# Expert value rows summed on TensorE in four 64x64 parts of the array, and more of them

## The reference

```python
vals, idx = lax.top_k(sc, PEER_TOPK)
...
experts = jnp.take_along_axis(cand_idx.reshape(...), top_c, axis=-1)
g = jax.nn.softmax(top_s, axis=-1)
ue = peer_u[experts]
ve = peer_v[experts]
act = jax.nn.gelu(jnp.einsum('td,thkd->thk', hc, ue).astype(jnp.float32), approximate=False)
return jnp.einsum('thk,thkd->td', (g * act).astype(ve.dtype), ve)
```

## Time and profile before

| | |
|---|---|
| Runs | 2926.47, 2927.46 (median), 2927.74 us |
| Profiled execution | one of these executions: span 2927.4 us, which lies within the three runs; next to nothing lies around it |
| Busy: PE, PEld | 2491.4 us (85%), 1743.2 us (60%) |
| Busy: DVE, ACT, POOL | 1760.7 us (60%), 1133.8 us (39%), 676.9 us (23%) |
| DMA | 838.64 MB, mean 286 GB/s |
| First dot product, last V row's sum | 567.2 us, some 2312 us |
| Before, in and behind the expert stage | 567, 1748 and 612 us |

### The profile page before, as it was taken

One profiled execution on the slowest core, in us unless ns is written; L12 is line 12 of the kernel. 1 busy time (PEld: TensorE's weight loads), 2 busy tenths in 40 slices (PEclk: granted clock), 3 DMA queues, 4 the chain that ended last, 5 costly groups with the idle time before them and its releaser, 6 DMA issues.

```text
span 2927.4 us, 29566 instructions
## 1 busy us (share of the span) xinstructions
PE 2491.4 (85%) x10118; PEld 1743.2 (60%) x10118; DVE 1760.7 (60%) x4222; ACT 1133.8 (39%) x2762; POOL 676.9 (23%) x566
## 2 busy tenths in 40 slices
PE   8999999879989759888968678588985799988998
PEld 7786666667755437546736544264763376655883
DVE  2101311598797778666989888878998416412430
ACT  2101301242533765354442578464554325512210
POOL 0000000122234343332223445444223101100000
PEclk9999999989989889999989578799997999999999
DMA  5545243689999999999899989999999743432443
GB/s 197 173 154 168 95 144 129 219 335 351 390 394 417 409 397 392 419 389 384 299 332 402 365 301 385 396 420 419 417 418 416 277 159 109 151 130 88 153 155 116
DMA packets 160966, 838.64 MB, mean 286 GB/s; under 512 B 17400, under 2 KB 21896, under 8 KB 95024
## 3 DMA queue, kind: packets, MB, share of 16 engines
q0 software_dynamic: 73728, 536.90, 45.8%
q1 hardware_dynamic: 82464, 287.75, 28.0%
q10 hardware_dynamic: 4624, 12.11, 1.1%
HBM read 828.27 MB, written 8.41 MB: 286 GB/s over the span
## 4 chain that ended last, share of the span: by engine, by line
PE 55%; DVE 18%; ACT 12%; DMA 11%; issue 4%; POOL 0%; ACTq 0%; DVEq 0%; SPq 0%
PE ps L908 26%; DMA BIG<-in_uv,BIG 10%; PE ps L928 5%; PE ps L929 5%; PE ps L1152 5%; DVE BIG L1943 5%; DVE X L1923 4%; PE ps L909 4%; PE ps L1176 2%; PE ps L1177 2%; ACT L1441 2%; DVE BIG L1854 1%; PE ps L1122 1%; DVE BIG L1851 1%; PE ps L1101 1%
## 5 line engine op out<-in xcount | busy, mean ns | idle before, releaser
L2160 POOL DMA_INDIRECT BIG<-in_uv,BIG x512 | 634.2, 1239 | 1646.3 <-DVE BIG L1900 564.6
L908 PE MATMUL ps<-BIG,RING 128*128 128x256 f32 x3472 | 807.6, 385 | 13.8 <-DMA RING<-in_w_cq 4.9
L908 PEld LDWEIGHTS ps<-BIG,RING 128*128 128x128 f32 x3472 | 670.1, 194 | 133.4 <-issue 28.6
L1943 DVE CUSTOM_DVE_ANT_0 BIG<-BIG 128x1024 f32<-128x1024 f32 x512 | 619.6, 1217 | 85.4 <-DMA BIG<-in_uv,BIG 84.2
L1923 DVE SCALAR_TENSOR_TENSOR X<-BIG,small,X 128x1024 f32<-128x1024 f32 x333 | 426.6, 1281 | 91.7 <-ACT small L1445 91.6
L1441 ACT ACTIVATE small<-small 128x1 f32<-128x1 f32 x512 | 102.6, 200 | 620.7 <-DVE small L1943 619.4
L908 PE MATMUL ps<-WK,RING 128*128 128x256 f32 x1232 | 287.2, 385 | 25.2 <-DVE BIG L1702 23.2
L908 PEld LDWEIGHTS ps<-WK,RING 128*128 128x128 f32 x1232 | 235.7, 193 | 65.3 <-DVE BIG L1702 31.1
L928 PE MATMUL ps<-RING,BIG 128*128 128x512 f32 (+1 forms) x448 | 223.0, 579 | 5.0 <-DVE BIG L1681 2.4
L929 PE MATMUL ps<-RING,BIG 128*128 128x512 f32 (+1 forms) x448 | 222.6, 578 | 0.0
L1274 ACT ACTIVATE BIG<-ps 128x256 f32<-128x256 f32 (+2 forms) x143 | 56.8, 398 | 408.5 <-PE ps L909 343.2
(11 more groups left out here) (259 smaller groups left out, 3136.7 us busy)
## 6 DMA issues: line engine op xcount, KB each, us to landing
RING<-in_w_up SPq DMA_DIRECT2D x88, 512.0 KB, 6.0
RING<-in_w_down SPq DMA_DIRECT2D x66, 512.0 KB, 3.6
RING<-in_w_pq SPq DMA_DIRECT2D x32, 512.0 KB, 6.1
RING<-in_w_cc SPq DMA_DIRECT2D x16, 512.0 KB, 8.1
RING<-in_w_cx SPq DMA_DIRECT2D x16, 512.0 KB, 4.1
RING<-in_w_cb SPq DMA_DIRECT2D x16, 512.0 KB, 4.4
RING<-in_w_cv SPq DMA_DIRECT2D x16, 512.0 KB, 5.0
RING<-in_w_gc SPq DMA_DIRECT2D x16, 512.0 KB, 4.7
```

The source lines that it names most:

```text
L908: e.matmul(ps[:, 0:256], W[:, j, :], src[:, j, 0:256], start=j == 0, stop=False)
L1943: e.tensor_tensor_reduce(out=u, in0=HF[:, t % 2, :], in1=u, scale=1.0, scalar=0.0, op0=ALU.mult, op1=ALU.add, accum_out=dots[:, k % 8:k % ...
L2160: e.indirect_dma_start(out=slot[i], out_offset=None, in_=I["uv"], in_offset=bass.IndirectOffsetOnAxis(ap=IDX[:, t, c:c + 1], axis=0)).then ...
```

## The change

The matmul of a V row is cut into four: for each half of the 128 tokens (partitions 0 to 63 and 64 to 127, rows of the array) and each half of the 1024 columns of the V row, one matmul of 64 tokens by 512 columns with a 64x64 diagonal. The four use four different quarters of the array: the token half gives the rows, and the token half exclusive-or the column half gives the columns, and with them the PSUM partitions. Token half 0 accumulates in bank 6, token half 1 in bank 7. The diagonal is made from a new `ident2` of 128x64, in which both halves of the partitions hold a 64x64 identity, and there are eight such buffers in place of four in the same memory. `total` adds four pieces of 64x512 in place of two of 128x512. The planner gives TensorE three rows in four in light stretches and until the selection of tile 1 is finished, and one in two in dense stretches after it; together 311 rows in place of 179.

```diff
--- before.py
+++ after.py
@@ -456,9 +456,9 @@
                         late.remove(j)
                         yield 0, "add", j
                 late.append(k)
-                if not self.norming and (self.light or (1, 3) not in self.chosen):
+                if not self.norming:
                     n += 1
-                    if n % 3 if self.light else n % 2:
+                    if n % 4 if self.light or (1, 3) not in self.chosen else n % 2:
                         self.pe_sums[t].append(k)
                 if c == 1 and t % 2:
                     yield 0, "total", t - 1
@@ -501,6 +501,7 @@
         small = sb("small", [128, 640])
         rb = sb("rb", [32, 8])
         DG = sb("DG", [128, 2, 128])
+        ident2 = sb("ident2", [128, 64])
         banks = [ctx.enter_context(nc.psum_tensor(f"ps{i}", [128, 512], F32)) for i in range(8)]
         scratch = nc.dram_tensor("bias_scratch", [8, 640], F32, kind="Internal")
         heads = nc.dram_tensor("head_scratch", [8, 128, 1024], F32, kind="Internal")
@@ -585,7 +586,7 @@
         dots = small[:, 480:488]
         acts = small[:, 488:496]
         ROOM = at_(W0 + 15360, 512)
-        DIAG = [DG[:, 0, :], DG[:, 1, :], at_(W0 + 15872, 128), at_(W0 + 16000, 128)]
+        DIAG = [DG[:, i // 2, 64 * (i % 2):64 * (i % 2) + 64] for i in range(4)] + [at_(W0 + 15872 + 64 * i, 64) for i in range(4)]
 
         K0 = W0 + 4096
         KN = at_(K0, 4, 512)
@@ -1171,10 +1172,14 @@
                 if k == pe_sums[t][0] and t and pe_sums[t - 1]:
                     w.wait_ge(*at["total", t - 1])
                 w.wait_ge(*at["gate", k])
-                v, d = slot[slot_of[k]][:, 1024:2048], DIAG[pe_turn[k] % 4]
+                v, d = slot[slot_of[k]], DIAG[pe_turn[k] % 8]
                 first, last = k == pe_sums[t][0], k == pe_sums[t][-1]
-                e.matmul(banks[6][:, :], d, v[:, 0:512], start=first, stop=last)
-                e.matmul(banks[7][:, :], d, v[:, 512:1024], start=first, stop=last).then_inc(pacc.sem, pacc("sum", k))
+                for side in range(2):
+                    for half_of in range(2):
+                        rows, to = slice(64 * half_of, 64 * half_of + 64), 64 * (half_of ^ side)
+                        mm = e.matmul(banks[6 + half_of][to:to + 64, :], d[rows, :],
+                                      v[rows, 1024 + 512 * side:1536 + 512 * side], start=first, stop=last)
+                mm.then_inc(pacc.sem, pacc("sum", k))
 
             def prepare():
                 ps = bank("b0")
@@ -1447,10 +1452,10 @@
                 n = pe_turn[k]
                 e.activation(a, a, ACT.Copy, scale=GS[:, t, c:c + 1]).then_inc(act.sem, act("gated", k))
                 own()
-                w.wait_ge(*at["ident"])
-                if n >= 4:
-                    w.wait_ge(*at["sum", pe_order[n - 4]])
-                e.activation(DIAG[n % 4], ident[:, :], ACT.Copy, scale=a).then_inc(gate.sem, gate("gate", k))
+                w.wait_ge(*at["ident2"])
+                if n >= 8:
+                    w.wait_ge(*at["sum", pe_order[n - 8]])
+                e.activation(DIAG[n % 8], ident2[:, :], ACT.Copy, scale=a).then_inc(gate.sem, gate("gate", k))
 
             def final_in(tag, h):
                 for name in final_start(tag, h):
@@ -1928,10 +1933,13 @@
                 w.wait_ge(acc.sem, acc.n)
                 if pe_sums[t]:
                     w.wait_ge(*at["sum", pe_sums[t][-1]])
-                    for hh in range(2):
-                        d = X[:, t, hh * 512:(hh + 1) * 512]
-                        e.tensor_tensor(d, banks[6 + hh][:, :], d, ALU.add).then_inc(dve.sem, dve("total", t))
-                        at["ev", "experts", 6 + hh] = (dve.sem, dve.n)
+                    for half_of in range(2):
+                        rows = slice(64 * half_of, 64 * half_of + 64)
+                        for side in range(2):
+                            to = 64 * (half_of ^ side)
+                            d = X[rows, t, 512 * side:512 * side + 512]
+                            e.tensor_tensor(d, banks[6 + half_of][to:to + 64, :], d, ALU.add).then_inc(dve.sem, dve("total", t))
+                        at["ev", "experts", 6 + half_of] = (dve.sem, dve.n)
                 else:
                     at["total", t] = (acc.sem, acc.n)
 
@@ -2171,6 +2179,13 @@
             w.wait_ge(*at["ident0"])
             e.affine_select(out=ident[:, :], in_=ident[:, :], compare_op=ALU.not_equal, fill=1.0, base=0, pattern=[[-1, 128]],
                             channel_multiplier=1).then_inc(pool.sem, pool("ident"))
+            e.memset(ident2[:, :], 0.0).then_inc(pool.sem, pool("ident20"))
+            w.wait_ge(*at["ident20"])
+            e.affine_select(out=ident2[:, :], in_=ident2[:, :], compare_op=ALU.not_equal, fill=1.0, base=0, pattern=[[-1, 64]],
+                            channel_multiplier=1).then_inc(pool.sem, pool("ident21"))
+            w.wait_ge(*at["ident21"])
+            e.affine_select(out=ident2[:, :], in_=ident2[:, :], compare_op=ALU.not_equal, fill=1.0, base=-64, pattern=[[-1, 64]],
+                            channel_multiplier=1).then_inc(pool.sem, pool("ident2"))
             w.wait_ge(*at["flip0"])
             e.affine_select(out=flip, in_=flip, compare_op=ALU.not_equal, fill=1.0, base=-127, pattern=[[1, 128]],
                             channel_multiplier=1).then_inc(pool.sem, pool("flip"))
```

## The result

The change made the kernel slower by a quarter of a percent: median 2933.47 us (2926.26 to 2939.10, 18 runs) against 2924.25 us (2919.07 to 2932.09, 18 runs) of before, ratio 1.0026 with a 95% interval of 1.0017 to 1.0034. By the ratio that is 7.6 us more, by the medians 9.2, where 11 us less were forecast. The profiled execution of after took 2926.26 us, the shortest of its 18, for a span of 2924.5; single executions of one kernel differ by 10 us and more, so where a profile and a median disagree by a few us, the median counts.

The account below looks back on a forecast made before the run. No engine was taken to bound the whole expert stage: DMA is full in some stretches, TensorE or VectorE leads in others. Terms of ten stretches sum to -11 us, from 2927.4 to 2916 us; range 2883 to 2990.

Parts of the forecast that it names:

- S8: Expert stage, V rows 357 to 409: DMA is full, so the change adds only 1 us.
- S6: Expert stage, V rows 256 to 298: VectorE loses 24 us, gathers at full DMA share allow at most 16: -14 us.
- S10: Last stretch of the expert stage: TensorE's V rows 32 to 19 us, half shows, longer total +1.4: -5 us.
- S9: Expert stage, stretch before the last: DMA full, but 15 rows fall where TensorE is dense: +4 us.
- rival 1: TensorE's V rows: column halves don't overlap, a row costs 2.1 us; 3026 us, or 2971 with half absorbed; chance 0.17.
- S1: Expert stage, V rows 0 to 76: TensorE's added work +2, VectorE's relief -8: -6 us.
- S3: Expert stage, V rows 154 to 181: 13 rows alone add 16.5 us where TensorE fills 81.4 of 89: +14 us.
- S7: Expert stage, V rows 299 to 356: TensorE 67 to 44, VectorE -5, a fifth of it shows: -6 us.
- S2: Expert stage, V rows 77 to 153: DMA full, nine rows come into dense work (+11), half shows: +4 us.
- S4: Expert stage, V rows 182 to 228: TensorE +6, VectorE -15, DMA share 0.98: +2 us.
- Rival 2: 871 to 928 us, S3, S4, 2035 to 2141 us: TensorE becomes the bound although four parts overlap; 2944 us, chance 0.15.
- Rival 3: Expert stage: no change, VectorE's relief ends at the DMA share (S1 -3, S6 -8, S7 -3); 2928 us, chance 0.19.

Follow-up runs that it names:

- TensorE's time alone: Four parts with the old rule, plus TensorE matmuls with zero weights for 97 dense rows that VectorE still sums: 2933.51 us, 1.0031 to the kernel before.
- sums two rows later: Kernel with four parts and 274 rows on TensorE, 91 dense rows summed four rows behind the dot product instead of two: 2943.48 us, 1.0058 to before.
- the 95 dense rows: Four parts with the old rule, plus one in two of the dense rows on TensorE (274 rows): 2926.80 us, 1.0007 to the kernel before.
- the 179-row kernel: The changed kernel's four parts with the planner's old rule, the same 179 rows on TensorE as before: 2907.98 us, 0.9943 to the kernel before.

## Why the prediction was wrong, point by point

Two steps failed, both about the dense rows: S8, where a full DMA share was taken for slack on TensorE (+1 forecast, +17.2 measured, by the profiled pair), and S6, where VectorE's relief was priced at -14 and -2.2 came. Two smaller ones, in S10 and in the first half of S9, nearly cancelled.

**The price of a row was right at the full clock.** All four parts at once, 1.21 us alone where 1.27 was forecast; rival 1 (column halves don't overlap) is out. The Trainium skill, TensorE: Matmul & The Clock Gate, What overlaps and what doesn't, on which rival 1 drew, states that a weight load overlaps a running matmul only on other rows. The trace shows otherwise, and the measurement decides: in the row above, the weight loads of the second passes begin some 0.05 us after the first passes have begun over the same rows, and all eight passes end 1.09 us after they begin. The Trainium skill, TensorEngine Tiling (Array Packing), Key Properties, states that a change of the tiling mode drains TensorE; the trace agrees, as a row alone takes 0.35 us beyond its two passes' 0.86. With the old rule the four parts alone gave 17 to 18 us.

**S1, S3 and S5 came as summed**: -5.8, +12.3 and -4.5 in the profiled pair, where -6, +14 and -5 stood. S1 did so in its parts too: the four parts alone gave 10 us, and the 20 rows more took back 4 to 7. S3 is TensorE's chain with 13 rows more:

```profile
by line: PE ps L909 46.2%; PE ps L929 14.6%; PE ps L930 13.6%; DMA RING<-in_w_cq 12.2%; PE ps L1180 11.1%; PE ps L910 6.9%; DVE X L1638 0.7%; DVE BIG L1684 0.4%; DVE BIG L1686 0.4%; issue 0.4%; SPq L825 0.3%; SPq L70 0.0%
```

**S6 is a step that failed**: "VectorE -24, but at full share ... at most -16: -14". The profiled pair shows -2.2. Leaving the sums out with nothing in their place gave 7.5 us, so the -14 was too large even for VectorE's relief alone; the bound that I took from the DMA share is not reached (0.97 where 1.02 is full). With one row in two of this stretch on TensorE 4.5 of them were left (light stretches at three in four), and in the changed kernel 2.2. GpSimd waited 70.8 us there for VectorE's slots before, and after 46.5 us for TensorE's and 36.1 for VectorE's. The runs point at held slots for the rest: TensorE's time alone cost this stretch 1.6 us, and sums two rows later 7.8. It is not shown for the change itself, since no run took the slots apart in this stretch by itself.

**S8 is the other: "DMA full: +1".** By itself it went from 147.2 to 164.4 us (V rows 357 to 409), +17.2, while S7 (299 to 356) gave 12.4 where 6 were forecast. Together the forecast was -5 and the pair shows +4.8; the 95 dense rows alone add 6.8 to the 179-row kernel there, and TensorE's time alone adds 10.5. I had let a full DMA share stand for slack on TensorE. In V rows 357 to 383 there was next to none, and the chain of waits of the kernel before, where no gather is among the entries shown, would have said so:

```profile
by line: PE ps L928 17.7%; PE ps L929 17.4%; DVE X L1923 13.8%; issue 10.4%; PE ps L908 9.8%; ACT BIG L1254 8.8%; ACT L1441 3.2%; ACT WK L1223 2.9%; DVE BIG L2089 2.2%; DVE BIG L1943 2.1%; ACT L1228 1.6%; ACT BIG L1245 1.3%; PE ps L896 1.2%
```

Busy time and TensorE's waits there, in the kernel before:

```profile
1838.00:1917.00 79.00, 44.61 (x135) 26.79 (x136) 69.53 (x102) 34.30 (x101) 38.68 (x27) 0.74 1.00 400
```
```profile
PE ps L896 <- DVE BIG L2089: 23.2, 1, 23.2
PE ps L896 <- ACT BIG L1245: 8.0, 1, 8.0
```

44.6 us busy and 31.2 us of waits for the norm of the mixed output are 76 of 79 us. That idle time stands in series with the work: when TensorE's time alone was added, it stayed at 30 us (30.1 and 29.6). After the change the same two sum to 87.5 of 90:

```profile
1820.00:1910.00 90.00, 51.36 (x184) 27.47 (x181) 62.25 (x94) 36.58 (x107) 44.05 (x26) 0.77 0.86 354
```
```profile
PE ps L897 <- DVE BIG L2097: 30.0, 1, 30.0
PE ps L897 <- ACT BIG L1250: 6.1, 1, 6.1
```

Of the 12 us here 6.8 are work and 4.9 a longer wait. TensorE's time alone explains some 5 (78.7 to 83.5 us). The rest is not shown; the chain of the changed kernel has GpSimd's gathers in it here (17%, and 10% for waits on their data), which speaks for slots that came free late.

The cover of the prediction had the same fault: "359 us in which TensorE is idle in the stage" counted such waits as room. The 97 dense rows' 107 us of TensorE time cost 26 us with no relief in return, VectorE's relief gives back 8 to 11, and the real dense rows cost 19. If these simply add, an estimate from the three runs, about 1 to 4 us are left for gates and held slots, the terms that the prediction put at 0.

**S2 and S4** were 6 and 3 us better in the pair than summed. **S9 and S10** together were 2 better by luck: V rows 425 to 454 took 5.1 us less where +4 stood, for a reason that stays open, and 455 to 510 3.6 us more where -5 stood. For S10 the prediction had TensorE's V rows fall from 32 to 19 us; after the change they took 41.5 there, at a granted clock of 0.57, which no term of the sum had. Over the stage the pair shows -1.6 us where -11 stood. The profiled execution of before lies 3 us over its median and that of after 7 us under its own, which makes up for the distance to the measured +7.6 to +9.2, and I can't assign it to a stretch.

**Rival 2** (TensorE becomes the bound in the dense stretches) is what happened in mechanism, but in one of its four places only: S3. The start of S2 (V rows 77 to 94) added 2.5 us of its 11, S4 (-1.0) and 2035 to 2141 (V rows 425 to 454, -5.1) none, and S8, where it happened as well, it didn't name. So its time, 2944, was too high. It had 0.15 where the forecast had 0.46. The price at which the sign turns was given as 1.23 us, 0.09 over my average; a sign which hangs on 8% of one price called for even chances. **Rival 3**'s mechanism, that the relief of VectorE passes only where the DMA share is under full, fits S6, where the share rose from 0.91 to 0.97 and 7.5 us came: 104 us of relief over all dense stretches were worth 8 to 11.

## What to carry to other kernels

Making an operation cheaper and giving more work to the engine that does it are two changes: here the first gave 17 to 18 us and the second took 25. Before work is moved to an engine, take its chain in each stretch: where busy time and the waits of its own chain filled the stretch, nearly every microsecond added showed (14 of 15 in S3), whatever another resource's share said; where the giving engine didn't end the stretch, next to none of its relief showed. Put the work where the taking engine has room and the giving one sets the pace; here 17 rows more in the light stretches took the kernel to 0.9908.

## What the runs showed of the hardware

That four 64x64 parts of the array take float32 passes at once, two column halves over the same 64 partitions of moving data among them, was not shown by any row of before. Where the change left TensorE less busy its granted clock fell: in S7 from 0.83 to 0.69 and in S10 from 0.83 to 0.57, as its busy time went from 140.7 to 127.0 and from 48.5 to 43.1 us. A pass of a 64x64 part with 512 columns lasts 589 or 640 ns at the full clock (2.4 GHz) and 1057 or 1112 at the lower level (1.2 GHz). Passes of 1 us and more are 107 of 716 in the kernel before, 580 of 2488 in the changed one and 566 of 1432 in the 179-row kernel, where the mean of a pass is 795 to 822 ns:

```profile
L1180 PE MATMUL ps<-BIG,DG 64*64 64x512 f32 x728 | 128.7, 795 | 88.7 <-ACT DG L1458 88.0
...
L1180 PE MATMUL ps<-BIG 64*64 64x512 f32 x704 | 128.5, 822 | 51.0 <-ACT BIG L1458 50.8
```

So part of what the four parts save in the light stretches goes back at the lower of the clock's two levels, which no term of the sum had: a row's passes took TensorE 1.07 us in S3 (granted clock 0.99), 1.6 in S7 and 1.9 in S10. It is not what made the dense rows cost: S3 kept 0.99, and in V rows 357 to 383 the clock rose from 0.74 to 0.77.
